# A gated-delta scan whose first two steps load their corner blocks from ScalarE's queue

## Chip, cores and metric

The kernel runs on one core of one Trainium2 chip. The metric is the device time of one execution in microseconds (us). SyncE (SP in the rows) only issues DMAs and waits; ScalarE (ACT), VectorE (DVE) and TensorE (PE) compute; ScalarE's instruction stream can issue DMAs too, on a queue of its own (q10 in the profile, where SyncE's is q1).

## The reference, cut to what matters

The program computes two transformer blocks in a row, on 512 latent tokens (and 256 context tokens that only feed the states). The first block mixes tokens with two recurrent head groups, each in both directions. The change lies in one of them, the gated delta rule:

```
def gdn_scan(q, k, v, g, beta, S0, return_y):
    ...
    kk = jnp.einsum('bchik,bchjk->bchij', k_beta, kc) * decay
    tmat = (jnp.eye(Q, dtype=jnp.float32) + jnp.where(strict, kk, 0.0)).astype(jnp.float32)
    ...
    sol = lax.linalg.triangular_solve(tmat, rhs, left_side=True, lower=True, unit_diagonal=True)
    u, w = sol[..., :V], sol[..., V:]
    ...
    def step(S, inp):
        u_i, w_i, kd_i, d_i = inp[:4]
        v_new = u_i - jnp.einsum('bhqk,bhkv->bhqv', w_i, S)
        S_next = S * d_i[..., None, None] + jnp.einsum('bhqk,bhqv->bhkv', kd_i, v_new)
        ...
```

For every chunk of tokens a unit triangular matrix has to be inverted (or solved with), and then a state is carried from chunk to chunk. 8 heads and 2 directions are scanned.

## The kernel before, in words

The work runs in stages: input projections (to about 518 us), a state-space scan on all engines with the 32x32 diagonal inverses computed on VectorE beside it (to 709 us), the gated-delta scan (709 to 955 us), norms, and then a long row of projections, MLPs and attention that TensorE fills (to 2690 us). The stages are parted by `barrier`, a semaphore `phase_end` that four engines drain into and wait on.

The gated-delta scan has 6 steps (t = 0 to 5, one chunk of 128 tokens each; `NCH = 6`). Each step has four groups q = 0 to 3: q // 2 is the direction, q % 2 selects four of the eight heads. A tile named X[q] is 128x512: four 128x128 blocks, one for each head. The inverse of the 128x128 triangular matrix is put together from its four 32x32 diagonal inverses:

- `DT[t % 2][q]` holds the diagonal inverses (SyncE's `load_dt`, line 760, four DMAs), `DB[q]` their transposes (`load_d32`, line 765, three DMAs), `C5[q]` the two 32x32 corner pieces of the matrix beside the diagonal (`load_corners`, line 772, two DMAs), and `C6[q]` the 64x64 corner (line 774, one DMA). `VB[q]` holds the values (`load_step`, line 783). All are read back from DRAM scratch. (In the profile C5 and C6 are both "C", and DT's first buffer is named DU.)
- TensorE's `corner5` waits until all ten of these DMAs of (t, q) have landed (`pre_loaded[q]` at 160 * (t + 1)) and for t > 0 until `dt_ready` of step t - 1, and multiplies C5 by DB. ScalarE copies the result to `PM[q]` (`corner`, line 1630). TensorE's `block5` multiplies it by DT; VectorE puts pieces into DB and DT. `corner6` (C6 by DB), another `corner` copy on ScalarE, `block6_t`, and a VectorE copy into DT (`dt_ready`) finish the inverse. All four products are the helper `four` (line 1071).
- A corner buffer of the next step may be loaded once `corner6` of this step has read it, so that the loads of (t, q) wait for `p6_full` at 4 * (t - 1) + q + 1.

The order is written out by hand on each engine. TensorE runs `corner5`, `block5`, `corner6`, `block6_t` of step 0, each for q = 0 to 3. Then, for each t, it runs `state_read(t, q)` and `corner5(t + 1, q)` for q = 0 to 3 (at t = 0 only the latter), `new_values(t, q)` and `block5(t + 1, q)`, `state_step(t, q)` and `corner6(t + 1, q)`, `key_rows(t + 1, q)` and `block6_t(t + 1, q)`. SyncE, an in-order stream, runs for t = 0 after barrier 2: `load_d32(0, q)` and `load_corners(0, q)` for each q (with a wait for GpSimd's zeroing of C5 and C6), then `load_step(0, q)`; and for t = 1 to 5 and each q: a wait for `p5_full`, `load_dt`, a wait for `p6_full`, `load_d32`, `load_corners`; then `load_step(t, q)`, which for t = 1 waits for TensorE's `new_values(0, q)` (`dr_full`). `load_dt(0, q)` runs earlier, beside the stage before.

ScalarE at the start of the scan: four small activations, one DMA that stores the 2 MB tile `yfm` to `y_scratch` (line 1623), two waits for earlier stores, four `corner` copies after `corner5`, four after `corner6`, and then the loop over t.

Of the kernel before, what the change touches and what calls it, by code (L numbers as in the profile page):

```python
# [231 lines left out]
def build_kernel(nc, a, out):  # L232
    ctx = ExitStack()
    with ctx:
# [3 lines left out]
        def at(name, kb, shape, dt=F32):  # L238

            tensors[name] = nc.alloc_sbuf_tensor_at(name, [shape[0], int(np.prod(shape[1:]))], dt, offset=base + int(kb * 1024))  # L240
            return tensors[name]
# [4 lines left out]
        def sem(name):  # L246
            return ctx.enter_context(nc.semaphore(name))
# [152 lines left out]
        def split_lo(dve, u, k, kc):  # L400

            dve.wait_ge(hi_ready, u + 1)
            if not isinstance(u, int) or u >= 2:
# [28 lines left out]
        S, DB, DT1, C5, C6 = ([at(f"{n}{q}", 36 + 8 * i + 2 * q, (P, 512)) for q in range(4)]  # L432
                             for i, n in enumerate(("S", "DB", "DT1", "C5", "C6")))
# [21 lines left out]
        pre_loaded = [sem(f"pre_loaded{q}") for q in range(4)]  # L455
        vb_loaded = [sem(f"vb_loaded{q}") for q in range(4)]
        qkd_loaded = [sem(f"qkd_loaded{q}") for q in range(4)]
        at_stored = [sem(f"at_stored{s}") for s in range(4)]
# [4 lines left out]
        at_dram = nc.dram_tensor("at_scratch", (4 * NCH, P, 512), F32).ap()  # L463
# [7 lines left out]
        def pair_of(q, t):  # L471

            return (q // 2 * NCH + GSEQ[q // 2][t]) * 2 + q % 2
# [5 lines left out]
        def block_at(q, t):  # L479

            if t < 4:
                return q // 2, (2 * t + q % 2) * 16
            return 2, 64 * (q // 2) + (2 * (t - 4) + q % 2) * 16
# [5 lines left out]
        def row_part(x, n):  # L489

            a = slice(x * P + 64 * n, x * P + 64 * n + 64)
            src = (g if x < 4 else eg)[:, :].rearrange("p (d c x) -> p d c x", d=2, c=NCH)
            c, h = ((0, 4), (SH, NH)) if x == 0 else ((2, 6), (SH, NH)) if x in (1, 6) else ((2 + 2 * (x % 2), 4 + 2 * (x % 2)), (0, SH))
            src = src[:, :, c[0]:c[1], h[0]:h[1]]
            if x in (2, 3):
                return src.rearrange("p d c h -> p c h d"), gparts[:, a].rearrange("p (c h d) -> p c h d", c=2, h=SH)
            return src.rearrange("p d c h -> p c d h"), gparts[:, a].rearrange("p (c d h) -> p c d h", c=c[1] - c[0], d=2)
# [104 lines left out]
        def ffn_jobs(l):  # L602
            return [(JOB[f"gu{l}{j}"], JOB[f"dn{l}{j}"]) for j in range(3)]

        width = [kc for _, kc, n, _ in JOBS for _ in range(n)]

        def next_width(u):
# [35 lines left out]
        def _(sp_):  # L643
# [87 lines left out]
            for ts, ds in (((0, 1, 2, 3), (0,)), ((0, 1, 2, 3), (1,)), ((4, 5), (0, 1))):  # L731
                for d in ds:
                    for t in ts:
                        for q in (2 * d, 2 * d + 1):
                            x, p0 = block_at(q, t)
# [21 lines left out]
            def load_dt(t, q):  # L757

                for r in range(4):
                    sp_.dma_start(diagonal(DT[t % 2][q][:, :], r), blocks_of(xb_dram, q, t, r)).then_inc(pre_loaded[q], 16)  # L760

            def load_d32(t, q):

                for r in (0, 1, 2) if q < 2 else (1, 2, 3):
                    sp_.dma_start(diagonal(DB[q][:, :], r), blocks_of(xv_dram, q, t, r)).then_inc(pre_loaded[q], 16)

            def load_corners(t, q):

                d, m = q // 2, at_dram[pair_of(q, t)]
                for src, dst in ((0, 1), (2, 3)) if d == 0 else ((1, 0), (3, 2)):  # L770
                    part = lambda x: x[32 * src:32 * src + 32, :].rearrange("i (j n) -> i j n", j=4)[:, :, 32 * dst:32 * dst + 32]
                    sp_.dma_start(part(C5[q][:, :]), part(m)).then_inc(pre_loaded[q], 16)
                half = lambda x: x[64 * d:64 * d + 64, :].rearrange("i (j n) -> i j n", j=4)[:, :, 64 - 64 * d:128 - 64 * d]
                sp_.dma_start(half(C6[q][:, :]), half(m)).then_inc(pre_loaded[q], 16)

            def load_step(t, q):

                d, c = q // 2, GSEQ[q // 2][t]
                if t == 1:
                    sp_.wait_ge(dr_full, q + 1)  # L780
                elif t > 1:
                    sp_.wait_ge(r_ready, 4 * (t - 2) + q + 1)
                sp_.dma_start(VB[q][:, :], v_dram[:, c * D + 512 * (q % 2):c * D + 512 * (q % 2) + 512]).then_inc(vb_loaded[q], 16)
                if t >= NCTX:
                    if t > NCTX:
                        sp_.wait_ge(o_full, 4 * (t - NCTX - 1) + q + 1)
                    sp_.dma_start(QKD[q][:, :], qk_dram[lat_pair(q, t)]).then_inc(qkd_loaded[q], 16)
# [8 lines left out]
            sp_.wait_ge(db_zeroed, 4)  # L796
            for q in range(4):
                load_d32(0, q)
                sp_.wait_ge(zeroed, 4 + 2 * (q + 1))
                load_corners(0, q)  # L800
            for q in range(4):
                load_step(0, q)
            for t in range(1, NCH):
                for q in range(4):
                    if t == 4:
                        sp_.wait_ge(xb_stored, 48)
                        sp_.wait_ge(xv_stored, 48)
                    n = 4 * (t - 1) + q + 1
                    if t == 1:
                        sp_.wait_ge(zeroed, 12 + q + 1)  # L810
                    else:
                        sp_.wait_ge(dr_full, n - 4)
                    sp_.wait_ge(p5_full, n)
                    load_dt(t, q)
                    sp_.wait_ge(p6_full, n)
                    load_d32(t, q)
                    load_corners(t, q)
                for q in range(4):
                    load_step(t, q)

# [592 lines left out]
        def _(act):  # L1413
# [73 lines left out]
            for u in range(job.n + 2):  # L1487
# [51 lines left out]
                if u == 15:  # L1539
                    act.wait_ge(gp_ready, 2)  # L1540
                    for x in range(7):
                        src, dst = row_part(x, 0)
# [84 lines left out]
            def corner(t, q, full):  # L1627

                act.wait_ge(full, 4 * t + q + 1)
                act.activation(PM[q][:, :], A[q][:, :], ACT.Identity, scale=-1.0).then_inc(pm_ready, 1)  # L1630

            def new_values(t, q):

                d, c = q // 2, GSEQ[q // 2][t]
                act.wait_ge(dr_full, 4 * t + q + 1)
                for j in range(4):
                    o = c * 16 + d * 8 + 4 * (q % 2) + j
                    ins = act.activation(VN[q][:, j * P:(j + 1) * P], B[q][:, j * P:(j + 1) * P], ACT.Identity, scale=beta[:, o:o + 1])
                ins.then_inc(nv_ready, 1)

            act.wait_ge(xb_stored, 48)
            act.wait_ge(xv_stored, 48)
            for q in range(4):
                corner(0, q, p5_full)
            for q in range(4):
                corner(0, q, p6_full)
            for t in range(NCH):
                more = t < NCH - 1
                if more:
                    for q in range(4):  # L1650
                        corner(t + 1, q, p5_full)
                for q in range(4):
                    new_values(t, q)
                if more:
                    for q in range(4):
                        corner(t + 1, q, p6_full)
# [224 lines left out]
        def _(dve):  # L1881
# [379 lines left out]
            def split_tmp(items, rs_done=False):  # L2261

                tps = work[sets[0]][2]
                n = len(items)
                for i in range(n + 1):
                    if i < n:
                        if t_n[0] >= 2:
                            dve.wait_ge(t_lo, t_n[0] - 1)
                        items[i][0](tps[t_n[0] % 2][:, :]).then_inc(t_ready, 1)
                        t_n[0] += 1  # L2270
                    if i >= 1:
                        m = t_n[0] - (1 if i == n else 2)
                        _, hi, lo, bias = items[i - 1]
                        dve.wait_ge(t_hi, m + 1)
                        dve.wait_ge(t_ready, m + 1)
                        t = tps[m % 2][:, :]
                        if bias is None:
                            dve.tensor_tensor(lo, t, hi.bitcast(F32), ALU.subtract).then_inc(t_lo, 1)  # L2278
                        else:
                            dve.scalar_tensor_tensor(out=lo, in0=t, scalar=bias, in1=hi.bitcast(F32), op0=ALU.add,  # L2280
                                                     op1=ALU.subtract).then_inc(t_lo, 1)
# [336 lines left out]
```

## Time and profile before

| | |
|---|---|
| median of 3 runs | 2705.18 us (2703.74 to 2710.03) |
| the profiled execution's own time | 2705.83 us |
| its span, first to last instruction | 2703.8 us |
| TensorE busy | 2492.8 us, 92% of the span |
| mean granted TensorE clock | 0.929 |
| the gated-delta scan | about 709 to 955 us |

The time is 2.03 us above the span; the rest of the profile is read inside the span. A granted clock of 1.00 is 2.4 GHz and 0.50 is 1.2 GHz. In the rows, "[3.29 <-DMA C<-at_scratch]" says that the engine sat idle for 3.29 us before the instruction and what ended it. SPq and ACTq are the DMA issues of the two queues, with the time that the issue took, not that of the transfer.

### The profile page before, as it was taken

The page shows a single profiled execution, that of the slowest core. Times are in us where ns is not written, and L with a number is a line of the kernel's source. Part 1 is how long each engine was busy: PE and PEld are TensorE (multiplying, and loading weights), DVE is VectorE, ACT ScalarE, POOL GpSimd, SP SyncE. Part 2 cuts the span into 40 slices and gives each one's busy share as a digit, 9 for nine tenths or more (in the row PEclk, how much of TensorE's full clock was granted, in tenths as well). Part 3 has the DMA queues.
Part 4 walks back from the last instruction along what each step waited for, and adds up shares of the span by engine and source line. Part 5 has one row for each costly group of instructions (what it writes and reads, how often), then busy time and mean ns, then how long its engine had stood idle before and what let it go on. Part 6 is the DMA issues. An engine that isn't in the chain of part 4 may idle for free.

```text
span 2703.8 us, 30593 instructions
## 1 busy us (share of the span) xinstructions
PE 2492.8 (92%) x12077; PEld 2013.3 (74%) x12077; DVE 1409.9 (52%) x2288; ACT 988.4 (37%) x1650; POOL 153.8 (6%) x116
## 2 busy tenths in 40 slices
PE   3899999888778979899999889999999999999997
PEld 2788877544578878688888766888888767888886
DVE  8557764587635653444434564443444464444445
ACT  3445557432122132323325434422224444422222
POOL 0000000000000001000003130100001120100002
PEclk8989999855589959899999999999999999999998
DMA  5233425401232232222223210222223210222222
GB/s 226 102 117 117 164 90 187 141 12 36 75 73 57 72 134 78 78 94 101 94 94 108 76 49 7 95 94 101 94 99 103 76 49 16 94 94 101 94 101 78
DMA packets 124302, 248.30 MB, mean 92 GB/s; under 512 B 58048, under 2 KB 58816, under 8 KB 123520
## 3 DMA queue, kind: packets, MB, share of 16 engines
q1 hardware_dynamic: 117360, 230.09, 25.0%
q10 hardware_dynamic: 6800, 16.25, 1.6%
q8 instruction: 96, 1.57, 0.2%
q14 instruction: 46, 0.38, 0.0%
HBM read 221.13 MB, written 25.17 MB: 91 GB/s over the span
## 4 chain that ended last, share of the span: by engine, by line
PE 60%; DVE 2%; ACT 2%; issue 0%; ACTq 0%; POOL 0%; DVEq 0%
PE bank L1220 17%; PE bank L1221 17%; PE bank L1222 17%; PE bank L1360 2%; PE bank L1351 2%; PE bank L1386 1%; PE bank L1203 1%; PE bank L1214 1%; DVE wlo L2334 0%; ACT whi L1707 0%; PE bank L1241 0%; ACTq L1676 0%; DVE tt L2370 0%; PE bank L1311 0%; DVE ylo L2278 0%
## 5 line engine op out<-in xcount | busy, mean ns | idle before, releaser
L1707 ACT ACTIVATE whi<-raw 128x1024 fp32r<-128x1024 f32 (+1 forms) x267 | 277.8, 1041 | 951.6 <-PE bank L1222 945.8
L1220 PE MATMUL bank<-ahi,whi 128*128 128x512 f32 x1152 | 454.5, 394 | 8.8 <-DVE alo L2375 5.9
L1221 PE MATMUL bank<-alo,whi 128*128 128x512 f32 x1152 | 450.2, 391 | 0.0
L1222 PE MATMUL bank<-ahi,wlo 128*128 128x512 f32 x1152 | 450.0, 391 | 0.0
L2334 DVE TENSOR_TENSOR wlo<-raw,whi 128x1024 fp32r<-128x1024 f32 (+1 forms) x267 | 326.1, 1221 | 156.5 <-ACT whi L1707 156.2
L1220 PE MATMUL bank<-bhi,whi 128*128 128x512 f32 x736 | 286.6, 389 | 0.0
L1222 PE MATMUL bank<-bhi,wlo 128*128 128x512 f32 x736 | 286.3, 389 | 0.0
L1221 PE MATMUL bank<-blo,whi 128*128 128x512 f32 x736 | 286.3, 389 | 0.0
L1220 PEld LDWEIGHTS bank<-ahi,whi 128*128 128x128 f32 x1152 | 217.6, 189 | 59.7 <-issue 11.3
L1221 PEld LDWEIGHTS bank<-alo,whi 128*128 128x128 f32 x1152 | 217.7, 189 | 45.9 <-issue 1.4
L1222 PEld LDWEIGHTS bank<-ahi,wlo 128*128 128x128 f32 x1152 | 217.4, 189 | 45.7
L2552 POOL TENSOR_TENSOR accx<-accx,sqr 128x512 f32<-128x512 f32 x42 | 72.3, 1721 | 1693.3 <-ACT sqr L1717 1469.3
L1220 PEld LDWEIGHTS bank<-bhi,whi 128*128 128x128 f32 x736 | 138.2, 188 | 29.0 <-issue 0.3
L1222 PEld LDWEIGHTS bank<-bhi,wlo 128*128 128x128 f32 x736 | 138.2, 188 | 28.7
L1221 PEld LDWEIGHTS bank<-blo,whi 128*128 128x128 f32 x736 | 138.2, 188 | 28.5
L2346 DVE TENSOR_TENSOR xr<-bank,xr 128x512 f32<-128x512 f32 x64 | 44.3, 692 | 159.6 <-PE bank L1222 159.6
L405 DVE TENSOR_TENSOR wlo<-raw,whi 128x1024 fp32r<-128x1024 f32 x51 | 62.3, 1222 | 99.7 <-ACT whi L398 99.6
L920 PE MATMUL bank<-hhi,whi 128*128 128x512 f32 x272 | 109.6, 403 | 0.0
L920 PE MATMUL bank<-hlo,whi 128*128 128x512 f32 x272 | 108.9, 400 | 0.0
L920 PE MATMUL bank<-hhi,wlo 128*128 128x512 f32 x272 | 108.3, 398 | 0.0
L398 ACT ACTIVATE whi<-raw 128x1024 fp32r<-128x1024 f32 x51 | 54.4, 1068 | 147.0 <-DMA raw<-in_s_qkvx 75.9
L1964 DVE SCALAR_TENSOR_TENSOR cacc<-cbuf,vec,cacc 128x784 f32<-128x784 f32 (+1 forms) x102 | 98.2, 963 | 10.7 <-ACT cacc L1502 8.0
(411 smaller groups left out, 4160.6 us busy)
## 6 DMA issues: line engine op xcount, KB each, us to landing
raw<-in_s_gu SPq DMA_DIRECT2D x88, 512.0 KB, 3.2
raw<-in_s_qkvx SPq DMA_DIRECT2D x34, 512.0 KB, 4.6
late_modw<-in_w_mod SPq DMA_DIRECT2D x32, 512.0 KB, 3.6
raw<-in_s_up SPq DMA_DIRECT2D x32, 512.0 KB, 3.2
raw<-in_s_down SPq DMA_DIRECT2D x32, 512.0 KB, 3.2
raw<-in_s_dn SPq DMA_DIRECT2D x32, 512.0 KB, 3.2
raw<-in_s_win SPq DMA_DIRECT2D x24, 512.0 KB, 3.2
raw<-in_s_zg SPq DMA_DIRECT2D x16, 512.0 KB, 4.0
```

What stands on the lines that cost most here:

```text
L398: act.activation(whi[k][:, 0:kc * P], raw[k][:, 0:kc * P], ACT.Identity).then_inc(hi_ready, 1)
L405: dve.tensor_tensor(wlo[k][:, 0:kc * P], raw[k][:, 0:kc * P], whi[k][:, 0:kc * P].bitcast(F32), ALU.subtract).then_inc(lo_ready, 1)
L920: mm = pe.matmul(lat, w, x[:, s, CTX:TOK], start=first, stop=last)
L1220: pe.matmul(out, w_hi, x_hi, start=start, stop=False)
L1221: pe.matmul(out, w_hi, x_lo, start=False, stop=False)
L1222: return pe.matmul(out, w_lo, x_hi, start=False, stop=stop)
L1351: pe.matmul(bank[m % 3][:, :], qh[:, h * LAT + qb * P:h * LAT + (qb + 1) * P], blk(kh, h), start=True, stop=True).then_inc(s2_full, 1)
L1360: mm = pe.matmul(bank[4 + (h // 2) % 2][64 * (h % 2):64 * (h % 2) + 64, qb * P:(qb + 1) * P], vh[:, kb_ * LAT + h * 64:kb_ * LAT + (h + 1) ...
L1707: act.activation(whi[u % 2][:, 0:width[u + 2] * P], raw[u % 2][:, 0:width[u + 2] * P], ACT.Identity).then_inc(hi_ready, 1)
L1964: after(dve.scalar_tensor_tensor(out=acc, in0=x, scalar=w, in1=acc, op0=ALU.mult, op1=ALU.add))
L2334: dve.tensor_tensor(wlo[u % 2][:, 0:width[u + 2] * P], raw[u % 2][:, 0:width[u + 2] * P], whi[u % 2][:, 0:width[u + 2] * P].bitcast(F32), ...
L2552: pool.tensor_tensor(acc[:, :], acc[:, :], sqr[n % 2][:, :], ALU.add).then_inc(sq_added, 1)
```

## The change

The corner transfers of t = 0 and t = 1 (for each t and q two of 32 rows for C5 and one of 64 rows for C6: 24 in all) leave SyncE's stream and are issued by ScalarE. Those of t = 0 come right behind the store of `yfm` and ahead of the first `corner` copy, each q behind the same wait for GpSimd's zeroing, with four waits for stores that ended long before. Those of t = 1 are issued for each q right behind the `corner(0, q, p6_full)` copy, which has waited for `p6_full`. Sizes, buffers, semaphores and all other waits stay. From t = 2 on SyncE loads the corners as before.

```
--- before.py
+++ after.py
@@ SyncE
             for q in range(4):
                 load_d32(0, q)
-                sp_.wait_ge(zeroed, 4 + 2 * (q + 1))
-                load_corners(0, q)
             for q in range(4):
                 load_step(0, q)
...
                     load_d32(t, q)
-                    load_corners(t, q)
+                    if t > 1:
+                        load_corners(t, q)
                 for q in range(4):
                     load_step(t, q)
@@ ScalarE
+            def load_corners(t, q):
+
+                d, m = q // 2, at_dram[pair_of(q, t)]
+                for src, dst in ((0, 1), (2, 3)) if d == 0 else ((1, 0), (3, 2)):
+                    part = lambda x: x[32 * src:32 * src + 32, :].rearrange("i (j n) -> i j n", j=4)[:, :, 32 * dst:32 * dst + 32]
+                    act.dma_start(part(C5[q][:, :]), part(m)).then_inc(pre_loaded[q], 16)
+                half = lambda x: x[64 * d:64 * d + 64, :].rearrange("i (j n) -> i j n", j=4)[:, :, 64 - 64 * d:128 - 64 * d]
+                act.dma_start(half(C6[q][:, :]), half(m)).then_inc(pre_loaded[q], 16)
+
+            for s in range(4):
+                act.wait_ge(at_stored[s], 16 * 6)
+            for q in range(4):
+                act.wait_ge(zeroed, 4 + 2 * (q + 1))
+                load_corners(0, q)
             act.wait_ge(xb_stored, 48)
             act.wait_ge(xv_stored, 48)
             for q in range(4):
                 corner(0, q, p5_full)
             for q in range(4):
                 corner(0, q, p6_full)
+                load_corners(1, q)
```

## Rows read from the trace of the kernel before

**Rows 1.** The page: busy us by engine, share of the span, instructions.

```profile
PE 2492.8 (92%) x12077; PEld 2013.3 (74%) x12077; DVE 1409.9 (52%) x2288; ACT 988.4 (37%) x1650; POOL 153.8 (6%) x116
```

**Rows 2.** Waits from 710 to 765 us: total us, times, longest.

```profile
PE bank L1071 <- DMA C<-at_scratch: 20.0, 7, 5.7
```

**Rows 3.** Timeline of the start of the scan, 680 to 722 us.

```profile
710.89 0.33 ACTq L1623 DMA_DIRECT2D y_scratch<-yfm  x1
...
712.23 2.92 SPq L765 DMA_DIRECT2D DB<-xv_scratch  x3
...
715.19 1.91 SPq L772 DMA_DIRECT2D C<-at_scratch  x2
...
717.14 0.60 SPq L774 DMA_DIRECT2D C<-at_scratch  x1
```

**Rows 4.** Timeline of steps 0 and 1, 715 to 762 us.

```profile
719.48 2.04 PE L1071 MATMUL bank<-DB,C 128*128 128x128 f32 x8 [5.67 <-DMA C<-at_scratch]
...
727.56 0.60 SPq L774 DMA_DIRECT2D C<-at_scratch  x1
...
730.00 2.07 PE L1071 MATMUL bank<-DB,C 128*128 128x128 f32 x8 [1.59 <-DMA C<-at_scratch]
...
731.87 5.26 PE L1071 MATMUL bank<-PM,DU 128*128 128x128 f32 x32
...
736.96 3.74 PE L1071 MATMUL bank<-DB,C 128*128 128x128 f32 x32
...
738.05 1.30 SPq L765 DMA_DIRECT2D DB<-xv_scratch  x3
738.05 0.60 ACT L1630 ACTIVATE PM<-bank 128x512 f32<-128x512 f32 x1 [5.35 <-PE bank L1071]
...
739.39 1.20 SPq L772 DMA_DIRECT2D C<-at_scratch  x2
...
741.33 1.97 SPq L760 DMA_DIRECT2D DT<-xb_scratch  x4
...
744.11 1.06 PE L1071 MATMUL bank<-DB,C 128*128 128x128 f32 x8
...
754.07 1.38 SPq L765 DMA_DIRECT2D DB<-xv_scratch  x3
...
759.01 2.07 PE L1071 MATMUL bank<-DB,C 128*128 128x128 f32 x8 [3.29 <-DMA C<-at_scratch]
```

**Rows 5.** SyncE's issues of line 765, from 712 to 716 us.

```profile
L765 SPq DMA_DIRECT2D DB<-xv_scratch x3: 318/1251/1254, 712.2 to 713.9; - x3
...
DMA to landing us min/median/max: 3.9/5.1/5.3
```

**Rows 6.** DMA issues by line, 700 to 1050 us: count, KB, median to landing.

```profile
y_scratch<-yfm ACTq DMA_DIRECT2D x1, 2048.0 KB, 6.4
...
C<-at_scratch SPq DMA_DIRECT2D x24, 64.0 KB, 2.2
DB<-xv_scratch SPq DMA_DIRECT2D x72, 16.0 KB, 1.7
```

**Rows 7.** Windows: length, PE, PEld, DVE, ACT, POOL busy, clock, DMA share, GB/s.

```profile
730.00:735.00 5.00, 5.00 (x23) 5.00 (x24) 0.91 (x3) 0.60 (x1) 0.00 (x0) 0.50 0.67 214
735.00:737.00 2.00, 2.00 (x20) 2.00 (x19) 1.51 (x5) 0.00 (x0) 0.00 (x0) 0.99 0.00 0
```

**Rows 8.** An issue on ACTq inside a burst on SPq, and line 698 there and without.

```profile
425.99 0.33 ACTq L1581 DMA_DIRECT2D zg_scratch<-stg  x1
...
L698 SPq DMA_DIRECT2D at_scratch<-AT x2: 430/432/435, 425.8 to 426.3; - x2
...
L698 SPq DMA_DIRECT2D at_scratch<-AT x2: 432/432/432, 445.2 to 445.6; - x2
```

**Rows 9.** Timeline of DMA issues on ACTq behind the scan, 926 to 966 us.

```profile
957.04 0.60 ACTq L1675 DMA_DIRECT2D gateb<-zg_scratch  x1
957.67 6.64 ACTq L1676 DMA_DIRECT2D yb<-y_scratch  x1
```

## The prediction

> **What bounds the kernel now.** I read the page first: TensorE is busy 92% of the span [rows 1], so time can only be won where it idles or runs at the low clock. One such place is the gated-delta scan: the view of waits for the start of the scan, 710 to 765 us: TensorE's products of line 1071 waited seven times for the DMAs of the corner tiles, 20.0 us in all [rows 2]. The timeline shows where. In step 0 the four `corner5` products start at 719.48 and 730.00 at the ends, with a wait ahead of each; in step 1 at 744.11 and 759.01, the last one after 3.29 us idle [rows 4]. And it shows who is slow: while TensorE waits, SyncE never rests. It issues ten DMAs for each q, one after the other: in step 1 the d32 loads of q = 0 begin at 738.05, those of q = 3 at 754.07, which is 5.34 us for each q [rows 4]. The transfers themselves are small and land 1.7 us (d32) and 2.2 us (C6) after their issue [rows 6]. So the issue stream bounds these two steps, and neither bandwidth nor any computing engine does. TensorE's clock is the second thing to see: products separated by such gaps run at 0.50, 2.04 to 2.07 us for eight, against 1.06 us at the full clock [rows 4], and from 730.00 on, where TensorE no longer pauses, the clock comes back only at about 735 [rows 7].
>
> **Step 0, what goes and what it costs.** SyncE loses 12 issues. A q's corners cost it 1.20 us for the pair and 0.60 us for C6, with gaps 1.94 us (739.39 to 741.33 in the same code of step 1) [rows 4]. ScalarE gains them, free: its `corner` copies cannot start before `corner5(0, 0)` anyway. It issues from about 711.3, behind the store of `y_scratch` at 710.89 [rows 3]. That store takes 6.4 us, to 717.3 [rows 6], and while it runs an issue on SyncE took 1.25 us, and d32 landed only 3.9 to 5.3 us after its issue, at 717.5 to 717.8 [rows 5]. No row shows small loads behind such a store on ScalarE's queue. The bounds: 0.33 us, the store's own issue [rows 3], and 1.25 us each [rows 5]. I take 0.95 us until 717.3 (SyncE's corner pair took 1.91 us there [rows 3]) and 0.60 us after it [rows 9]: six issues by 717.3, six more by 720.9; the last C6 starts at 720.3 and lands 2.2 us later, at 722.5. SyncE's d32 for q = 0 end at 715.15 as before; three issues for q = 1 at 0.8 us, then six at 0.45 us, end at 720.3, and the last lands at about 721.6.
>
> TensorE: the first product starts when the store's tail and d32 are through, between 718.3 and 719.5; I take 718.9 (before: 719.48). The four then no longer wait: at the low clock (0.50) the next product follows after 1.87 us (730.00 to `block5` at 731.87 [rows 4]), so that `corner5(0, 3)` would start at 724.5, later than its data at 722.5, and `block5` at 726.4. Since TensorE runs on without a pause, the clock comes back about 5 us in (730.00 to 735 [rows 7]), at 724, and the 2.4 us behind it take half: `block5` begins at 725.2 (before 731.87), and its 32 products take 3.6 us, as those of `corner6` do (736.96 to 740.5), instead of 5.1 [rows 4]. `corner6` begins at 728.8 instead of 736.96: 8.2 us. Bounds from the two issue costs: with 0.33 us TensorE sets the pace alone and nothing changes; with 1.25 us until 717.3 and 1.0 us after, the last C6 lands at 726.5 and 5 us are won.
>
> **Step 1.** Call T0 the first `corner` copy after `corner6`, 738.05 before [rows 4]. SyncE reached the d32 loads of q = 3 at T0 + 16.0. Three corner sets of 1.94 us stand ahead of them no more: T0 + 10.2. Their third issue starts 0.95 us later and lands after 1.7 us [rows 6]: T0 + 12.8, against the start of `corner5(1, 3)` at T0 + 20.96 (759.01) [rows 4]. So 8.1 us.
>
> What the moved issues delay lies on ScalarE: three issues stand behind each copy to PM, ahead of the next copy, and TensorE's `block6_t` of the next q waits for that. At 0.60 us each [rows 9] the fourth copy starts at T0 + 5.5 and ends at T0 + 6.1, and `block6_t(0, 3)` starts there instead of T0 + 5.2; VectorE's copy and `corner5(1, 0)` follow at T0 + 7.0 instead of T0 + 6.06 (744.11) [rows 4]. The later three `corner5` would be through by T0 + 10, still ahead of the d32 loads of q = 3 at T0 + 12.8: nothing of this delay is paid, with 2.8 us of cover. If the cover were gone it would cost that 0.9 us. The last corner load of step 1 starts at T0 + 7.2 and lands at T0 + 9.4, hidden as well. What is late next is thus still SyncE, with d32 and DT.
>
> The clock: before, `corner5(1, 3)` (2.07 us) ran at the low clock and so did about 1.2 us behind it, some 3.2 us, of which half is lost [rows 4]. With one pause of about 2.7 us in place of three, the clock may hold or fall: 0 to 1.6 us, I take 0.8.
>
> **Behind it.** SyncE's loads for step 2 wait for `new_values(0, q)`, which follow `corner5(1, 3)`; SyncE is idle by then as before (its last issue of step 1 ends at T0 + 11.6). So the steps from t = 2 on, whose corners stay on SyncE, move as they are, and so does all behind the scan; nothing there waits for a fixed time.
>
> **Sum.** 8.2 + 8.1 + 0.8 = 17.1 us off the profiled execution's 2705.83 us, 2688.7. The median of the runs is 0.65 us lower, which is less than my error; I forecast 2688.5 us.
>
> **The rivals.** (a) Issues on the two queues share what makes them slow, so that moving them wins nothing. Then 24 issues in step 0 take what they took; only the earlier start on ScalarE (711.3 for 712.23) and the shorter landing of d32 against C6 (0.5 us) are won at each step: 1 to 3 us, 2703. For it: an issue alone takes 0.33 us, the next 0.6, as if something behind the issuing engine set the pace [rows 3, 9]. Against it: where ScalarE issued a store at 425.99, in the middle of a burst of SyncE's, its issue took 0.33 us and SyncE's next ones 430 and 435 ns, against 432 and 432 in a burst that it left alone [rows 8]. The Trainium skill, Perfetto Trace Analysis, section "DMA Instruction — HWDGE (DVE, Sync)", describes one descriptor-generating block behind a lock that sequencers share; by that rule the time would be that of (a), and this one burst does not bear it out.
>
> (b) Half of it: ScalarE's queue is held up behind the 2 MB store, or the clock stays low, while step 1 goes as forecast or nearly. A clock that stays low through step 0 takes 2.5 us, a late last corner 3, a fallen clock in step 1 0.8 and more: 6 to 12 us won, 2696.
>
> (c) Slower: ScalarE's issues are so slow that they become the path. With x us for an issue, the last corner of step 0 starts at 711.3 + 11 x and lands after 2.2 us, against 730.00, and in step 1 the fourth copy comes at T0 + 9 x and `corner5(1, 3)` at about T0 + 9 x + 4.5, against T0 + 20.96. Together 20 x - 33.0 us: even at x = 1.65, slower by more than 5.4 us from x = 1.92. At x = 2.1 it is 9 us, 2715. For it stands one issue of 6.64 us on this very queue, behind two 2 MB loads [rows 9]; against it 0.60 us for the one ahead of that, and 1.25 us as the worst under the store [rows 5].
>
> **How the numbers follow.** Forecast (13 to 20 us won, 2685 to 2692) 0.65; (b) 0.16; (a) 0.13; (c) 0.06. A measurement of this kernel can tell about 0.2%, 5.4 us, from no change: faster 0.65 + 0.16 less 0.02 for a (b) that ends just short of 5.4 us, 0.79; same 0.13 + 0.02 = 0.15; slower 0.06. The range reaches over the forecast and (b), 2684 to 2702, and leaves out (a) and (c), 0.19.
>
> **What would show it.** The profile after should have, in the first 12 us of the scan, issues of the corner lines on ACTq of 0.6 to 1.25 us; `corner5(0, q)` in a row without waits; `block5` near 725; each q of step 1 on SyncE 3.4 us instead of 5.34; copies to PM in step 0 that stand 1.8 us apart instead of 0.9; `corner5(1, 3)` 12 to 13 us behind T0, ended by a d32 load and not by a corner; and the waits of line 1071 for DMAs in steps 0 and 1 down from 20.0 us to about 8 (5.1 ahead of the first product, 2.7 ahead of `corner5(1, 3)`), with those of t = 2 to 5 unchanged. The prediction is wrong if SyncE's issues stretch while ScalarE issues, if the corners of q = 2 and 3 land after 725, or if the stages behind the scan give the gain back.

## The result, and the profile after

| | before | changed |
|---|---|---|
| median of the runs timed side by side (5 each) | 2705.18 us (2701.24 to 2710.03) | 2692.82 us (2689.37 to 2694.39) |
| the profiled execution: time, span | 2705.83, 2703.8 us | 2692.82, 2690.8 us |
| mean granted clock | 0.929 | 0.932 |

The ratio is 0.995, with a 95% interval of 0.9935 to 0.9965: 12.4 us faster by the medians, 13.0 us by the two spans. The interval is 9.5 to 17.6 us of the 2705.18. The forecast was 2688.5 us and 17 us won, in a range of 2684 to 2702.

The page of the changed kernel, busy time by engine:

```profile
PE 2488.0 (92%) x12077; PEld 2009.8 (75%) x12077; DVE 1407.4 (52%) x2288; ACT 988.4 (37%) x1650; POOL 153.4 (6%) x116
```

Its waits from 710 to 765 us (total us, times, longest), which answer to [rows 2]:

```profile
PE bank L1070 <- DMA DB<-xv_scratch: 8.8, 3, 5.1
```

TensorE now waits 8.8 us for DMAs instead of 20.0, and it is the d32 loads, not the corners, that end these waits. The timeline of the changed kernel, which answers to [rows 3] and [rows 4]:

```profile
707.72 0.47 PE L893 MATMUL bank<-cf,gparts 128*128 128x128 f32 x1 [0.72 <-ACTq L352]
...
709.21 2.10 ACTq L1645 DMA_DIRECT2D C<-at_scratch  x2
...
710.02 9.41 SPq L765 DMA_DIRECT2D DB<-xv_scratch  x12
...
716.75 6.67 PE L1070 MATMUL bank<-DB,C 128*128 128x128 f32 x32 [5.14 <-DMA DB<-xv_scratch]
...
718.71 0.62 ACTq L1647 DMA_DIRECT2D C<-at_scratch  x1
...
723.25 3.74 PE L1070 MATMUL bank<-PM,DU 128*128 128x128 f32 x32
...
727.91 0.60 ACT L1629 ACTIVATE PM<-bank 128x512 f32<-128x512 f32 x1 [3.87 <-PE bank L1070]
...
731.82 1.25 ACTq L1645 DMA_DIRECT2D C<-at_scratch  x2
...
733.91 2.52 SPq L760 DMA_DIRECT2D DT<-xb_scratch  x4
...
737.96 1.80 SPq L760 DMA_DIRECT2D DT<-xb_scratch  x4
...
739.80 1.38 SPq L765 DMA_DIRECT2D DB<-xv_scratch  x3
...
742.58 2.08 PE L1070 MATMUL bank<-DB,C 128*128 128x128 f32 x8 [1.82 <-DMA DB<-xv_scratch]
```

Read from the start of the scan (707.72 here, 709.92 before; it is the gate transpose behind barrier 2). The four `corner5` groups of eight products run as one block of 32 without a wait between them. The first copy to PM behind `corner6`, T0, comes 20.19 us into the scan (727.91 - 707.72) where it came at 28.13 us before: 7.94 us won. `corner5(1, 3)` starts 14.67 us behind T0 (742.58 - 727.91) where it was 20.96: 6.29 us. From there to the first `state_step` at 752.64 it is 10.06 us, and it was 9.72 before (768.73 - 759.01): 0.34 lost. The scan as a whole, from that transpose to the first load of the next stage, went from 245.50 us (709.92 to 955.42) to 231.35 us (707.72 to 939.07): 14.15 us. The rest of the difference of the spans is not the change's: the scan started 2.20 us earlier, and the stretch behind it took 1751.7 us instead of 1748.4. Over the spans of all ten kernels of this study the start of the scan lies between 705.91 and 710.57 us, and the stretch behind the scan between 1747.5 and 1752.4 us, in no order of what was changed. The length of the scan in one trace is therefore the sharper measure here, and the experiments below are read by it, beside the medians. It varies too, by about a microsecond: in the five kernels whose step 0 is that of the changed kernel (this one, e1_step0, e3_all, e5_no_corners1, e6_double1) T0 comes between 19.19 and 20.42 us into the scan; in the three with step 0 as before (before, e2_step1, e8_dummy) between 27.12 and 28.13. The means differ by 7.9 us, so the gain of step 0 does not hang on the two traces above.

One row of the same timeline shows something that no term of the prediction had: SyncE's four DT loads of a q take 2.52 us at 733.91, while ScalarE issues, and 1.80 us at 737.96, when it no longer does.

### The profile page after: what moved, and what is told of

It is laid out like the page before. It is cut to its first block, busy times and chain, and to the rows that moved or that the text cites. A ratio compares the mean times of both kernels' runs of the same rounds, so it can differ in the third digit from the quotient of the medians.

```text
span 2690.8 us, 30595 instructions
## 1 busy us (share of the span) xinstructions
PE 2488.0 (92%) x12077; PEld 2009.8 (75%) x12077; DVE 1407.4 (52%) x2288; ACT 988.4 (37%) x1650; POOL 153.4 (6%) x116
## 4 chain that ended last, share of the span: by engine, by line
PE 60%; DVE 2%; ACT 2%; issue 0%; ACTq 0%; POOL 0%; DVEq 0%
PE bank L1219 17%; PE bank L1221 17%; PE bank L1220 17%; PE bank L1359 2%; PE bank L1350 2%; PE bank L1385 1%; PE bank L1202 1%; PE bank L1213 1%; DVE wlo L2348 1%; ACT whi L1721 0%; PE bank L1240 0%; ACTq L1690 0%; PE bank L1310 0%; DVE tt L2384 0%; DVE ylo L2292 0%
## 5 line engine op out<-in xcount | busy, mean ns | idle before, releaser
L1219 PE MATMUL bank<-ahi,whi 128*128 128x512 f32 x1152 | 455.2, 395 | 10.1 <-DVE alo L2389 6.9
L1219 PEld LDWEIGHTS bank<-ahi,whi 128*128 128x128 f32 x1152 | 217.9, 189 | 61.0 <-issue 11.7
```

Source lines behind the costliest of these rows:

```text
L1219: pe.matmul(out, w_hi, x_hi, start=start, stop=False)
```

## Experiments

The first four ran side by side with the kernel before (median 2708.46 us over 18 runs on that chip), the last four likewise (2708.51 us over 7 runs). Scan lengths are from the start of the scan to the first issue of the next stage, as above, in one trace of each kernel.

### Each step alone

```
@@ e1_step0: SyncE, t > 0
-                    if t > 1:
-                        load_corners(t, q)
+                    load_corners(t, q)
@@ e1_step0: ScalarE
                 corner(0, q, p6_full)
-                load_corners(1, q)
@@ e2_step1: SyncE, t = 0
                 load_d32(0, q)
+                sp_.wait_ge(zeroed, 4 + 2 * (q + 1))
+                load_corners(0, q)
@@ e2_step1: ScalarE
-            for q in range(4):
-                act.wait_ge(zeroed, 4 + 2 * (q + 1))
-                load_corners(0, q)
```

> Only the corners of step 0 are issued by ScalarE; those of step 1 are back on SyncE. Theory A (the issue stream of SyncE set the pace, and each step's share of the gain is its own): step 0 gives the 7.9 us that the changed kernel's trace shows between the start of the scan and the first corner copy behind corner6, and step 1 is as before, so 7 to 9 us faster than the kernel before (about 2697). Theory B (the gain comes from the clock or from one step alone, for instance because step 1 only profits when TensorE enters it warm): the whole 12 us or nearly nothing.

> Only the corners of step 1 are issued by ScalarE. Theory A: corner5 of the last q starts 14 to 15 us behind the first corner copy that follows corner6, against 20.96 before: 5 to 7 us faster (about 2699), and this with the gain of step 0 alone adds up to that of both. Theory B: nothing, or all of it.

Measured: step 0 alone 2702.03 us (11 runs), ratio 0.9976 (0.9967 to 0.9986), some 6.5 us; scan 237.23 us, 8.3 us less than before. Step 1 alone 2700.49 us (7 runs), ratio 0.9974 (0.9959 to 0.9988), some 7.0 us; scan 239.20 us, 6.3 us less. The two add up to 14.6 us of scan against 14.15 for both, and by the ratios to 13.5 us against 13.5. So each step's gain is its own to about a microsecond, and the theory that all of it comes from one step or from a clock that one step hands to the next is out. By themselves the ratios leave 3.8 to 8.9 us for step 0 and 3.3 to 11.1 for step 1; it is the traces that part the two. In e2_step1 `corner5(1, 3)` starts 14.65 us behind T0, as expected. In e1_step0, where step 1 was expected as before, it starts at 21.96 us (747.42 - 725.46), 1.0 later than before: the first three d32 loads of step 1 took 1.88 us to issue instead of 1.30, with ScalarE issuing nothing, and no run says why.

### All six steps

```
@@ e3_all: SyncE
-                    if t > 1:
-                        load_corners(t, q)
@@ e3_all: ScalarE, in the loop over t
                         corner(t + 1, q, p6_full)
+                        if t + 2 < NCH:
+                            load_corners(t + 2, q)
```

> The corners of all six steps are issued by ScalarE, those of step t + 2 behind each corner copy that follows corner6(t + 1). Theory A: in the steps from t = 2 on TensorE waits 1 to 1.4 and 3.3 to 3.6 us for the corners at the last two q; SyncE's set per q falls from 5.4 to about 3.5 us, so these waits go, 4 to 5 us for each of 4 steps, 12 to 18 us beyond the changed kernel (about 2678). Rival C (ScalarE becomes the path: three issues of 0.62 us stand ahead of each next copy to PM, where the copies come 1.79 us apart): the copies slip and the gain is eaten, 0 to 5 us beyond the changed kernel or slower.

Measured: 2668.52 us (2666.53 to 2673.82), ratio 0.9857 (0.984 to 0.9873): 38.7 us faster than the kernel before and 25.3 us of scan beyond the changed kernel (206.04 us), above the expected 12 to 18. Windows over three whole steps, from one `state_read` that follows `gated_query` to the same one three steps on, of the changed kernel at 800.10 to 923.71 us and of this one at 794.42 to 900.65 us, show 41.2 and 35.4 us for a step. The timeline of the changed kernel has one long wait for corners in each of these steps (3.59, 3.33 and 3.41 us) and in two of them a short one ahead of it (0.19 and 0.64), for instance

```profile
892.92 1.67 PE L1070 MATMUL bank<-DB,C 128*128 128x128 f32 x8 [3.41 <-DMA C<-at_scratch]
```

and the window of this kernel over such steps (length, then PE, PEld, DVE, ACT and POOL busy, clock, DMA share, GB/s)

```profile
794.00:900.00 106.00, 105.07 (x925) 103.74 (x924) 66.52 (x181) 28.05 (x72) 0.00 (x0) 1.00 0.31 78
```

has TensorE busy for 105.07 of 106 us at the full clock. Over the three whole steps TensorE is idle for 12.1 us in the changed kernel and for 0.9 here, 3.7 us for a step; I had counted only that. The other 2.1 us are the same products taking 111.5 us busy instead of 105.3, with a granted clock of 0.96 instead of 1.00: the low clock behind a wait was part of the price of the wait. Rival C, that ScalarE becomes the path, is out: the copies that its issues push back cost nothing that the trace shows.

### The store of yfm behind the corners

```
@@ e4_y_later: ScalarE
-            act.dma_start(y_dram, yfm[:, :]).then_inc(y_spilled, 16)
...
                 load_corners(0, q)
+            act.dma_start(y_dram, yfm[:, :]).then_inc(y_spilled, 16)
```

> As the changed kernel, but the 2 MB store of yfm is issued by ScalarE behind the corners of step 0 and not ahead of them. Theory A (in the changed kernel the start of step 0 waits for that store: the first d32 loads land 3.9 to 5.3 us after issue while it runs): the first corner5 starts 2 to 3 us earlier after the start of the scan than 9.0 us, and the last data of step 0 come 1 to 2 us earlier: 1.5 to 3 us beyond the changed kernel (about 2690). Rival: the store only moves its load onto the later transfers (d32 of q = 2 and 3, VB), and nothing is won or up to 2 us lost.

Measured: 2697.49 us (2694.04 to 2701.3), ratio 0.9961 (0.9947 to 0.9975), against 0.995 (0.9935 to 0.9965) for the changed kernel: the two intervals overlap, and the medians alone do not part these kernels. The scan is 236.34 us, 5.0 us longer than the changed kernel's, and all of it has come by T0 (25.48 us into the scan instead of 20.19). The rival was right, and more than it said. Issues and products of this kernel from 707 to 728 us:

```profile
710.17 7.45 SPq L765 DMA_DIRECT2D DB<-xv_scratch  x12
...
713.61 4.98 PE L1070 MATMUL bank<-DB,C 128*128 128x128 f32 x24 [1.85 <-DMA DB<-xv_scratch]
...
716.92 0.61 ACTq L1653 DMA_DIRECT2D y_scratch<-yfm  x1
...
724.85 2.08 PE L1070 MATMUL bank<-DB,C 128*128 128x128 f32 x8 [6.25 <-DMA DB<-xv_scratch]
```

The first product does start early, 5.74 us into the scan instead of 9.03, so the store is what holds it in the changed kernel. But the last d32 load is issued just as the store is; it lands 7.8 us after its issue, and the fourth `corner5`, which waits for it, starts 7.2 us after SyncE's d32 issues have ended. The four VB loads behind it land 8.7 us (median) after their issue, against 3.6 in the changed kernel. In this one trace the store delays what is in flight beside it.

### Step 1 with ScalarE issuing nothing, and with it issuing twice as much

```
@@ e5_no_corners1
                 corner(0, q, p6_full)
-                load_corners(1, q)
...
-                pe.wait_ge(pre_loaded[q], 160 * (t + 1))
+                pe.wait_ge(pre_loaded[q], 160 * (t + 1) - (48 if t else 0))
@@ e6_double1, behind load_corners(1, q) of the changed kernel; e8_dummy, behind corner(0, q, p6_full) of the kernel before
+                for k in range(3):
+                    act.dma_start(spare[32 * q:32 * q + 32, :].rearrange("i (j n) -> i j n", j=4)[:, :, 32 * k:32 * k + 32],
+                                  at_dram[pair_of(q, 1)][32 * q:32 * q + 32, :].rearrange("i (j n) -> i j n", j=4)[:, :, 32 * k:32 * k + 32]).then_inc(spare_loaded, 16)
```

> As the changed kernel, but the corners of step 1 are not loaded at all (step 1 computes with step 0's corners; this part of the computation is left out), and corner5 of step 1 and later waits for 48 less. It measures step 1 with SyncE's stream alone. Theory D (issues on the two queues slow each other, and this made step 1 win 6.3 us and not 8.1): SyncE's d32 and DT issues take 1.38 and 1.8 to 2.0 us for each q throughout, and corner5 of the last q starts 12.5 to 13 us behind the first corner copy after corner6, not 14.7. Rival E (the prediction forgot something that SyncE waits for, with no tie to ScalarE's issues): 14 to 15 us as in the changed kernel.

> As the changed kernel, but ScalarE issues for each q of step 1 three more DMAs of 16 KB behind the three corner DMAs, into a tile that nobody reads. Theory D: the 12 issues of the changed kernel cost SyncE's stream 1.7 us, about 0.14 us each; 24 cost about 3.4 us, and corner5 of the last q starts 16 to 17 us behind the first copy, unless ScalarE's own copies set it: they now come 3.8 us apart, the fourth at 11.5 us, and the last corner set is issued by 13.4 us and lands at 15.6 us. Rival E: SyncE's own stream is as in the changed kernel, its last d32 issue begins at 12.8 us.

> The kernel before (all corners on SyncE), with 12 more DMAs of 16 KB issued by ScalarE in step 1, three behind each corner copy, into a tile that nobody reads. Theory D: SyncE's set of step 1 takes 1.5 to 2 us longer, corner5 of the last q starts at 22.5 to 23 us behind the first copy instead of 20.96. Rival E: 20.9 to 21.1 us.

These three were run once each, for their traces (2694.73, 2691.92 and 2711.37 us); their times by themselves show nothing. With nothing issued by ScalarE in step 1, T0, SyncE's last d32 loads and the last product are

```profile
730.99 0.60 ACT L1629 ACTIVATE PM<-bank 128x512 f32<-128x512 f32 x1 [3.87 <-PE bank L1070]
...
741.07 1.38 SPq L765 DMA_DIRECT2D DB<-xv_scratch  x3
...
743.76 2.08 PE L1070 MATMUL bank<-DB,C 128*128 128x128 f32 x8 [2.23 <-DMA DB<-xv_scratch]
```

SyncE's sets of four DT loads take 1.73 to 1.80 us there and those of three d32 loads 1.25 to 1.38. The last product starts 12.77 us behind T0 (743.76 - 730.99), inside what theory D expected, against 14.67. With twice the issues on ScalarE, the last part of the stretch:

```profile
740.41 2.51 SPq L762 DMA_DIRECT2D DT<-xb_scratch  x4
741.57 1.24 ACTq L1647 DMA_DIRECT2D C<-at_scratch  x2
...
742.96 1.91 SPq L767 DMA_DIRECT2D DB<-xv_scratch  x3
```

From the d32 loads of q = 1 on, every set of SyncE's is now the slow one. The start of its d32 loads for q = 3 behind T0 is the clean measure: 10.1 us with 0 issues on ScalarE (741.07 - 730.99), 11.9 us with 12 (739.80 - 727.91), 13.4 us with 24, of which 21 have gone out by then (742.96 - 729.56): 1.8 and 3.3 us. Three other kernels with 12 issues in this stretch (e2_step1, e3_all, e4_y_later) have 12.0, 11.9 and 12.1 us. (The 12.8 us that the expectation for e6 gives for rival E is the start of the last of the three d32 issues, 740.8 in the changed kernel; in e6_double1 it is 744.3, 14.7 us behind T0.) The product itself was not at 16 to 17 us but at about 18 (its copy to PM at 748.89, less the 1.09 us from such a product to its copy at the full clock): ScalarE's copies, 3.9 us apart, had become the path, as this row of e6_double1 says:

```profile
738.30 2.08 PE L1072 MATMUL bank<-DU,PM 128*128 128x128 f32 x8 [2.76 <-ACT PM L1631]
```

And with all corners on SyncE and 12 idle loads on ScalarE, the d32 loads of q = 3 start 17.4 us behind T0 (753.81 - 736.43) instead of 16.0, and the last product 22.3 us behind it instead of 20.96: 1.4 us, a little under the 1.5 to 2 expected. The scan of that kernel is 249.61 us, 4.1 more than before; 1.5 of it has come by the first `state_step`, and the rest, in the steps behind it, no run explains. Rival E, that SyncE waits for something with no tie to ScalarE's issues, is out: each of the three runs moved SyncE's stream the way theory D has it, and nearly by its amount.

What the scan makes of it is less. The scan lengths are 231.02 us with ScalarE silent, 231.35 in the changed kernel and 232.06 with twice the issues, but these hold the chance differences of step 0 as well (T0 at 20.42, 20.19 and 19.19 us). From T0 to the first `state_step` it is 23.76 us with ScalarE silent (754.75 - 730.99), 24.73 in the changed kernel and 26.27 with twice the issues (755.83 - 729.56): of the 1.9 us that the silent queue won at `corner5(1, 3)`, 1.0 us were left there. The other 0.9 are the clock's. The windows from `corner5(1, 3)` to the first `state_step`, of the changed kernel and of e5_no_corners1:

```profile
742.58:752.64 10.06, 10.06 (x72) 10.06 (x73) 2.74 (x9) 4.72 (x16) 0.00 (x0) 0.80 0.29 80
```

```profile
743.76:754.75 10.99, 10.99 (x73) 10.99 (x73) 2.74 (x9) 4.72 (x16) 0.00 (x0) 0.73 0.27 73
```

TensorE is busy throughout in both, with the same products, at a granted clock of 0.80 and of 0.73. Whether a silent ScalarE brings the lower clock is not shown: the same stretch took 10.55 us in e2_step1, 9.77 in e3_all and 9.64 in e4_y_later, whose step 1 is coded as in the changed kernel, and 9.51 in e1_step0.

### All corners on ScalarE, and the store behind step 0's products

```
@@ e7_best: ScalarE, on top of e3_all
-            act.dma_start(y_dram, yfm[:, :]).then_inc(y_spilled, 16)
...
                 corner(0, q, p5_full)
+            act.dma_start(y_dram, yfm[:, :]).then_inc(y_spilled, 16)
             for q in range(4):
                 corner(0, q, p6_full)
```

> All corners on ScalarE as in e3_all, and the 2 MB store of yfm is issued behind the four corner5 copies of step 0, when the small loads of step 0 have landed. Theory A with the store as the thing that holds step 0's start: corner5 starts 5.5 to 6.5 us after the start of the scan instead of 9.0 and is then paced by SyncE's d32 loads of 1.4 us each, so that step 0 wins 2 to 3 us: about 2666. Rival: the store now runs beside VB and the DT loads of step 1 and delays them; new_values of step 0 waits for VB, and nothing is won or some us lost (2668 to 2673).

Measured: 2666.56 us (2663.97 to 2670.28), ratio 0.9856 (0.9833 to 0.988); scan 204.91 us against 206.04 for e3_all. The first product starts 5.6 us into the scan, as expected, and step 0 wins what was expected: T0 comes at 16.97 us instead of 19.50. But the rival has a part too: from T0 to the first `state_step` it is 25.71 us instead of 24.32, for SyncE's issues of step 1 are slower (four DT loads 2.71 us instead of 2.16 in the first set), and its d32 loads for q = 3 start 12.8 us behind T0 instead of 11.9. So only 1.1 us of scan are left at the end, and the ratios of the two (0.9857 and 0.9856) cannot be told apart. Both kernels are 25 us of scan or more ahead of the changed one; nearly all of that is the corners of t = 2 to 5.

## Why the prediction was right, point by point

**The number.** The forecast was 17 us won; 12.4 came by the medians (9.5 to 17.6) and 14.15 in the scan. The median, 2692.82 us, lies a little outside the forecast's own 2685 to 2692 and inside the stated range, which reached over rival (b) too. But what (b) named did not happen: the granted clock was back at 1.00 from 723 us, before `block5`, and ScalarE's 12 issues took 10.1 us for a forecast of 9.6. What did happen is a part of rival (a).

**What bounds these steps** was read rightly: the issue stream of SyncE. Taking 12 issues out of it won 8.3 us in step 0 alone and 6.3 in step 1 alone, and the waits of TensorE went from the corners to the next thing on that stream, d32.

**Step 0: 8.2 us forecast, 7.94 measured.** Into the scan, the forecast had `corner5` at 9.0 us and `block5` at 15.3; they came at 9.03 and 15.53. ScalarE's 12 issues ran from 709.21 to 719.33, 10.1 us for a forecast of 9.6. SyncE's 12 d32 issues took 9.41 us, to 11.7 us into the scan, where I had 10.4. Only part of this is the store: without it they took 7.45 us (e4_y_later), 0.62 us each and not 0.45, while ScalarE issued. The error was hidden because TensorE's own pace was later still, but not by much: in e6_double1, whose step 0 is the same and whose clock came back earlier, the fourth `corner5` waited 0.19 us for its d32 load.

```profile
723.90 1.16 PE L1072 MATMUL bank<-DB,C 128*128 128x128 f32 x8 [0.19 <-DMA DB<-xv_scratch]
```

That is 13.5 us into the scan; I had that load landing at 11.7. The price of a slower ScalarE in the prediction also holds a slip: with 1.25 us until 717.3 and 1.0 us after it, the last C6 starts at 723.5 and lands at 725.7, not 726.5.

**Step 1: 8.1 us forecast, 6.29 measured. This is the term that was mis-sized.** The prediction held that with the three corner sets gone SyncE would reach the last d32 loads at T0 + 10.2 and the product would start at T0 + 12.8. With ScalarE silent that is just what happens (10.1 and 12.77 us, e5). With ScalarE issuing, SyncE is 1.8 us later. I had kept SyncE's issue times of a stream that runs alone. That is the cause of 1.8 of the 3.2 us that the forecast was too high inside the scan; it does not say that its removal would bring them, since in e5 the clock took back half. The prediction had named this as a sign of being wrong, "if SyncE's issues stretch while ScalarE issues", and the sign came: it was right in its number and in what bounds the steps, and wrong in this step. Rival (a), that the two queues share what sets the pace, was thus neither right nor out: it was true for part of the cost, and (a)'s own time (2703 us) was wrong since the two queues together issue a small load every 0.31 us or so, and SyncE's alone one every 0.45. The burst in [rows 8] had a single issue of ScalarE in it, too few to show this.

**The clock: 0.8 us forecast, 0.34 lost.** `corner5(1, 3)` still ran at the low clock (2.08 us for eight, as before), behind two waits of 1.8 us; the clock had fallen by then. So the term fell outside its bounds of 0 to 1.6, on the other side of nothing. The same stretch took 9.72 us before at a granted clock of 0.83, 10.06 in the changed kernel at 0.80, and between 9.51 and 10.99 in all these kernels but e6_double1, which came into it at the full clock: it varies by more than a microsecond, which a forecast of 0.8 could not resolve.

**What ScalarE's issues delay** was put at nothing, with cover. The copies came 1.96 us apart (1.8 forecast) and `block6_t(0, 3)` waited 0.8 us for the last; in e5, where they are not delayed, `corner5(1, 3)` comes earlier by 1.9 us, and SyncE's d32 loads by 1.8, which leaves the copies next to nothing. The cover was real, and e6 shows a point beyond its end: at copies 3.9 us apart they are the path.

**Behind it.** That the steps from t = 2 on would only move was right: 13.9 us were won up to the first `state_step` and 14.15 by the end of the scan. The sum of the terms in the scan is 7.94 + 6.29 - 0.34 = 13.9 for a forecast of 17.1. The medians moved by 12.4 us; the sum lies in their interval, 9.5 to 17.6 us, and the stretches outside the scan differ by up to 5 us from one execution to the next.

## What to carry to other kernels

When TensorE waits for many small transfers, look whether the engine that issues them ever rests: if not, the count of its issues is the price, and moving some to another engine's queue can pay, here in each step separately. Reckon the other queue's issues as costing the first one something while both run (here 0.18 us for each of its own), and ask how far apart the copies on the engine that takes them over may come before they become the path. And a wait cured in two steps of six is worth looking for in the other four: here these held nearly twice as much.

## What the runs showed of the hardware

Issues on SyncE's and ScalarE's queues stretch each other, and unevenly. Alone, SyncE's small loads take 0.45 us each (four in 1.80 us, three in 1.38 us). While ScalarE issues at 0.62 us each, SyncE's take 0.63 us (2.51 us for four, 1.91 us for three), and ScalarE's are hardly longer than SyncE's corner loads alone (0.60 us). So both run at nearly the same pace, and together they put out an issue every 0.31 us or so. The Trainium skill, Perfetto Trace Analysis, section "DMA Instruction — HWDGE (DVE, Sync)", says that one block, locked for exclusive use, generates the descriptors for the sequencers that share it. If that lock were the whole of an issue's time, two streams would take turns and nothing would be won; the runs bear it out only as a stretch of 0.18 us for each of SyncE's issues. Whether it is that lock or something else behind the two queues that stretches them was not tried. Nor is it all that stretches an issue: e1_step0 has 1.88 us for three d32 loads with ScalarE silent.

The 2 MB store beside small loads was the other surprise: put 8 us later it did not cost less, it cost 5 us more of scan (e4), since a d32 load that is issued with it lands 7.8 us after its issue, against a median of 1.7 us over the scan before [rows 6]. Issued behind step 0's `corner5` products, it let step 0 win 2.5 us, and step 1 then took 1.4 us longer (e7 beside e3, one trace each).
